# Two transformer blocks on one core: side work of the mixer placed between the dense projection blocks, and the second block's modulation moved into the feed-forward

## The chip, the cores and the metric

The kernel runs on one core of a Trainium2 chip. The metric is the device time of one execution in microseconds (us); lower is better. Engines are named as the profile names them: PE (TensorE, matmul), PEld (its weight load), DVE (VectorE), ACT (ScalarE), POOL (GpSimd), SP (SyncE, which here issues all DMAs).

## The reference

The input is x, 512 tokens by 1024 channels, f32. `first_block` runs two layers; `second_block` runs one.

```
for l in range(2):                                 # first_block
    proj = rms_norm(x) @ w_in[l]                    # latents a, group B, C + indexer, group D
    A: latents cq (256), ckv (128): rms_norm, up-projection, rope, causal attention, 4 heads
    B: q 4 heads, k and v 2 heads, rope, window of 128 keys with a sink per head
    C: I[t,s] = sum_h w[t,h] relu(q_idx[t,h].k_idx[s]), top 128 keys, attention over them
    D: causal attention with a forget gate, cum = cumsum(log_sigmoid(f))
    x = x + concat(A, B, C, D) @ w_out[l]
    x = x + square(relu(rms_norm(x) @ w_up[l])) @ w_down[l]
x = rms_norm(x) * final_norm
shift, scale, gate = split(c @ w_ada + b_ada)       # second_block
h = rmsnorm(x) * (1 + scale) + shift
proj = h @ w_in_2                                   # three qkv groups, z, u, z_pool, gates
three dilated window attentions with a bias table rel_bias[bucket], merged by their lse
pool mixer, gated branches, x + gate * (merged @ w_out), rmsnorm
```

## The kernel before

**Dense products.** Every weight matrix is cut into jobs of 1024 x 512, a job into two pieces (halves of K). SP loads a piece into one of 4 slots of `raw`; ACT rounds it to `w_hi` (helper `ahead`, `split_high`), POOL subtracts to get `w_lo` (`split_low`, L1107, two instructions of 128x1024 a piece), and PE makes three matmuls for each block (`three`, L1637 to L1639). `product` (one job) runs half 0 over four token tiles into four PSUM banks `G`, then half 1; each bank is handed to ACT or DVE as it fills. `w_hi` and `w_lo` have two places.

**Order.** Each engine has one program, and programs meet at counted semaphores; an engine never passes a wait. In a layer PE does: transposes of x; `project(JOB_IDX)` (296 columns), `project(JOB_A)` (420); three turns of the indexer rows; `project(JOB_C)`; `index_products(1)` and `(2)`, three turns of the latents; `project(JOB_B)`; `index_products(3)`, the latents' up-projections (L1739, L1743); `project(JOB_D)`; the cumulated gates (L1753); `project(JOB_V)`. Between two products PE waits for what the other engines make of its small results: for the indexer, ACT applies relu from PSUM to `rel` (two places) and DVE multiplies and adds into `select` (L1459, L1462). DVE also does all ropes (`rotate`), the 32 rounds of `top_round` for query tiles 1 and 2 (MAX8 and MATCH_REPLACE8, L1490 and L1491) and, beside the attention, the 16 rounds of query tile 3.

**Attention.** 32 items (8 head pairs in the order D, B, A, C, times 4 query tiles) run in a software pipeline: scores, maximum (DVE), exponential (ACT), scaling by 1/sum (POOL, L1116), transposes, copy, output. One top-k round for tile 3 follows each of the first 16 items on DVE.

**Feed-forward.** Four groups of four jobs in a hardware loop: two up jobs, ACT relu, DVE square and split, two down jobs whose banks DVE adds to X (`add_to_x`, L1603).

**Second block.** It opens with six jobs ADA (c broadcast to 128 rows times `w_ada`), between them 24 matmuls of the bias lines (L874) that ACT copies to `stage`; two norms of X one after the other (final norm of the first block, written to X; then the norm for `xn2`); transposes of `xn2`; `h_full` (ACT, scale and shift), its split into `h_hi`, `h_lo` (L668, L669); then the first qkv job. SP writes `stage` to DRAM (4.6 MB) and reads the skewed bias tables back.

Of the kernel before, what the change touches and what calls it, by code (L numbers as in the profile page):

```python
# [15 lines left out]
P = 128  # L16
# [9 lines left out]
HD = 64  # L26
# [24 lines left out]
JOB_IDX, JOB_A, JOB_C, JOB_B, JOB_D, JOB_V = range(6)  # L51
# [13 lines left out]
TR_MLA = TR_IDX + 3  # L65
TR_CUM = TR_MLA + 3
TR_NORM2 = TR_CUM + 2
# [3 lines left out]
PAIRS = [(g, hp) for g in "DBAC" for hp in range(2)]  # L71
# [4 lines left out]
def qk_units(p):  # L76

    return 4 if PAIRS[p][0] in "DA" else 2
# [23 lines left out]
IDX_PRODUCTS = 3 * 8  # L102
SM_EXP = 0
LAYER_SM = SM_EXP + 2 * TT
LAYER_SC = NI
LAYER_OV = NI
assert LAYER_TR % 2 == 0 and LAYER_TURNS % 2 == 0 and LAYER_SM % 2 == 0
# [39 lines left out]
ADA = 0  # L147
QKV = 6
Z_JOB, U_JOB, ZP_JOB = 15, 16, 17
GATE_JOBS = 18  # L150
BRANCH = 22
OUT2 = 24
# [4 lines left out]
SM2_BIAS = DEPTH * LAYER_SM  # L157
SM2_POOL = SM2_BIAS + B2_HEADS
# [30 lines left out]
TR2_MOD = TR0  # L189
TR2_NORM = TR2_MOD + 4  # L190
# [50 lines left out]
UNITS_CREDIT, PAIR_CREDIT, IDX_CREDIT = TT, 2, 4  # L241

# [29 lines left out]
def build(nc, A, out):  # L272
    ctx = ExitStack()
    with ctx:
        def sem(name):
# [8 lines left out]
        skew_dram = nc.dram_tensor("skew_scratch", [B2_HEADS, P, SKEW], F32, kind="Internal").ap()  # L284
        merge_dram = nc.dram_tensor("merge_scratch", [SEQ, PACK], F32, kind="Internal").ap()
# [19 lines left out]
        top8 = base.place("top8", [P, 8])  # L305
        neg_max = base.place("neg_max", [P, 2, 2])
# [23 lines left out]
        fox_q, fox_k = (room.place(n, [P, TT, HEADS, FOX_K]) for n in ("fox_q", "fox_k"))  # L330
        mla_q, mla_k = (room.place(n, [P, TT, HEADS, MLA_QK]) for n in ("mla_q", "mla_k"))
        mla_v = room.place("mla_v", [P, TT, HEADS * HD])
        dead_at = room.at
        w_uq, w_ukv = room.place("w_uq", [P, 2, HEADS * MLA_QK]), room.place("w_ukv", [P, HEADS * 2 * HD])
        k_idx4 = room.place("k_idx4", [P, TT, 4 * 32])
        qiT, kiT = room.place("qiT", [P, 2, SEQ]), room.place("kiT", [P, SEQ])
        select = room.place("select", [P, (2 + 3 + 4) * P])
        work, rel = room.place("work", [P, SEQ]), room.place("rel", [P, 2, SEQ])
        turn = room.place("turn", [P, 4, 8 * HD // 2])
# [6 lines left out]
        ident_few, window_few = room.place("ident_few", [P, P], BF16), room.place("window_few", [P, 2 * P], BF16)  # L346

# [3 lines left out]
        relu, square = room.place("relu", [P, 2, SEQ]), room.place("square", [P, SEQ])  # L351

        room = Room(nc, free_at)
        xn2 = room.place("xn2", [P, TT, D_MODEL])
        cb_hi, cb_lo = room.place("cb_hi", [P, KT, P], F32R), room.place("cb_lo", [P, KT, P], F32R)
        h_full = room.place("h_full", [P, 2, SEQ])
        hot = room.place("hot", [P, 3, SKEW])
        stage_at = room.at
        stage = room.place("stage", [P, B2_HEADS, SKEW])
        rel_wide = room.place("rel_wide", [P, B2_HEADS, P])  # L360
# [4 lines left out]
        assert room.at <= stage_at  # L365
        room = Room(nc, stage_at)
# [10 lines left out]
        assert room.at <= last_at  # L377
        room = Room(nc, last_at)
        gate_row, gain_row = room.place("gate_row", [P, D_MODEL]), room.place("gain_row", [P, D_MODEL])
        rel_row = room.place("rel_row", [P, B2_HEADS])  # L380
        mod_b, mod = room.place("mod_b", [P, 2 * KT]), room.place("mod", [P, 2 * KT])
        norm_col, c_col, pool_gain = (
            room.place(n, [P, k]) for n, k in (("norm_col", KT), ("c_col", KT), ("pool_gain", 4)))
# [21 lines left out]
        inv_ready, prob_scaled = sem("inv_ready"), sem("prob_scaled")  # L405
        small_filled, small_drained = sem("small_filled"), sem("small_drained")
# [5 lines left out]
        m_sumsq_ready, m_var_ready, m_std_ready, m_rows_ready = (  # L412
            sem(n) for n in ("m_sumsq_ready", "m_var_ready", "m_std_ready", "m_rows_ready"))
# [4 lines left out]
        heads_ready = sem("heads_ready")  # L418
        rel_used, neg_max_ready, hidden_split = sem("rel_used"), sem("neg_max_ready"), sem("hidden_split")
        dve_step = sem("dve_step")  # L420
        b2_loaded, gain2_loaded, c_ready = sem("b2_loaded"), sem("gain2_loaded"), sem("c_ready")
        rel_ready, skew_saved, bias_loaded = (
            sem(n) for n in ("rel_ready", "skew_saved", "bias_loaded"))
# [11 lines left out]
        def weights2(job, half):  # L435

            if job < QKV:
                w, c0, k0 = A["w_ada_2"], 512 * job, half * HALF_K
            elif job < Z_JOB:
# [17 lines left out]
        def second_loads(sp):  # L457
            sp.wait_ge(tr_drained, TR0 + PAIR_CREDIT)
            column = lambda v: v.rearrange("(k p) -> p k", p=P)
            for dst, src in (  # L460
                (c_col[:], column(A["c_2"][0, :])),
                (rel_row[0:NUM_BUCKETS, :], A["rel_bias_2"]),
                (gain_row[:], A["final_norm"].unsqueeze(0).broadcast_to([P, D_MODEL])),
                (norm_col[:], column(A["norm_g_2"][0, :])),
                (mod_b[:], column(A["b_ada_2"][0, 0:2 * D_MODEL])),
                (gate_row[:], A["b_ada_2"][0:1, 2 * D_MODEL:3 * D_MODEL].broadcast_to([P, D_MODEL])),
                (pool_gain[:], column(A["pool_scale_2"][0, :])),
                (inv_count[:], c_count[:, :, :]),
            ):
                sp.dma_start(dst, src, allow_slow_non_contiguous=True).then_inc(b2_loaded, 16)  # L470
            for job in range(OUT2 + 2):
# [4 lines left out]
                if job == 1:  # L476

                    sp.wait_ge(bank_drained, UNIT0 + UNITS_CREDIT)
                    sp.dma_start(hot[0:NUM_BUCKETS + 1], c_hot[:, :, :]).then_inc(hot_loaded, 16)
                if job == QKV:  # L480

                    sp.wait_ge(small_drained, SM2_BIAS + B2_HEADS + PAIR_CREDIT)
                    sp.dma_start(skew_dram.rearrange("h p u -> p h u"), stage[:]).then_inc(skew_saved, 16)
                    sp.wait_ge(x_scaled, 1)
                    sp.dma_start(gain_row[:], A["final_g_2"].unsqueeze(0).broadcast_to([P, D_MODEL])
                                 ).then_inc(gain2_loaded, 16)
# [3 lines left out]
                    sp.dma_start(bias_near[:], skewed(0, B2_H, 0, 2 * P)).then_inc(bias_loaded, 16)  # L490
                if job == QKV + 7:
# [21 lines left out]
        def second_scalar(act, split_high, square_sums, square_roots):  # L513
# [18 lines left out]
            def bias_rows(job):  # L532

                for h in range(4 * job, 4 * job + 4):
                    act.wait_ge(small_filled, SM2_BIAS + h + 1)
                    act.activation(stage[:, h, :], S[:, h % 2, 0:SKEW], ACT.Copy).then_inc(small_drained, 1)
# [7 lines left out]
            ahead(ADA + 1, 0)  # L544
            act.wait_ge(x_scaled, 1)
            square_sums(xn2)
            square_roots(DEPTH + 1)
            ahead(ADA + 1, 1)
            bias_rows(1)
            for job in range(2, QKV):  # L550
                ahead(job, 0)
                ahead(job, 1)
                bias_rows(job)

# [7 lines left out]
            for gn, g in enumerate(B2_GROUPS):  # L562
                for s in range(3):
                    job = QKV + 3 * gn + s
                    ahead(job, 0)
                    if gn == 0 and s == 0:
                        act.wait_ge(skew_saved, 16)
# [45 lines left out]
            square_roots(DEPTH + 2)  # L613

        def second_vector(dve, step, root, normal_rows):
            dve.wait_ge(b2_loaded, 8 * 16)

            wide = c_col[:].unsqueeze(2).broadcast_to([P, KT, P])
            step.done(dve.tensor_copy(cb_hi[:], wide))
# [33 lines left out]
            for ins in scaled_rows(2 * DEPTH, DEPTH):  # L653
                pass
# [1244 lines left out]
```

## Time and profile before

| | |
|---|---|
| median of 3 runs | 2209.36 us (2195.4 to 2210.68) |
| the profiled execution | 2206.09 us, its span 2204.1 us |
| granted PE clock, mean | 0.932 of full speed |
| PE / PEld busy | 1976.2 / 1568.6 us (90% / 71%) |
| DVE / ACT / POOL busy | 957.9 / 666.0 / 798.4 us |
| HBM read | 161.85 MB, 77 GB/s |

Busy times are sums over instructions and overlap between engines. [...] The first layer's projections lie at 22.4 to 198.6 us of the span, its attention up to 332 us, its feed-forward up to 744 us; the second layer repeats this up to 1470.5 us; the second block follows.

### The profile page before, as it was taken

The page shows a single profiled execution, that of the slowest core. Times are in us where ns is not written, and L with a number is a line of the kernel's source. Part 1 is how long each engine was busy: PE and PEld are TensorE (multiplying, and loading weights), DVE is VectorE, ACT ScalarE, POOL GpSimd, SP SyncE. Part 2 cuts the span into 40 slices and gives each one's busy share as a digit, 9 for nine tenths or more (in the row PEclk, how much of TensorE's full clock was granted, in tenths as well). Part 3 has the DMA queues.
Part 4 walks back from the last instruction along what each step waited for, and adds up shares of the span by engine and source line. Part 5 has one row for each costly group of instructions (what it writes and reads, how often), then busy time and mean ns, then how long its engine had stood idle before and what let it go on. Part 6 is the DMA issues. An engine that isn't in the chain of part 4 may idle for free.

```text
span 2204.1 us, 23720 instructions
## 1 busy us (share of the span) xinstructions
PE 1976.2 (90%) x9164; PEld 1568.6 (71%) x9168; DVE 957.9 (43%) x1704; ACT 666.0 (30%) x1167; POOL 798.4 (36%) x366
## 2 busy tenths in 40 slices
PE   7789889999999977988999999988889898788986
PEld 6556557878778855755777878765688786666765
DVE  3567842322323346875241422332111223756773
ACT  4333443312212342344231222234332323221211
POOL 4223233344444431323334444457331322132441
PEclk9888999999999988989999999998898888898998
DMA  6212001222222331200122222334631132031210
GB/s 191 75 39 77 1 1 58 96 92 91 84 95 79 89 108 39 69 9 1 41 94 95 95 79 94 113 98 153 229 96 37 40 116 77 2 100 57 96 58 38
DMA packets 109520, 170.89 MB, mean 78 GB/s; under 512 B 21724, under 2 KB 39388, under 8 KB 109309
## 3 DMA queue, kind: packets, MB, share of 16 engines
q1 hardware_dynamic: 109436, 169.76, 24.1%
q8 instruction: 55, 0.90, 0.2%
q14 instruction: 29, 0.23, 0.0%
HBM read 161.85 MB, written 7.90 MB: 77 GB/s over the span
## 4 chain that ended last, share of the span: by engine, by line
PE 62%; issue 14%; DVE 10%; POOL 10%; ACT 3%; SPq 1%; DMA 0%; DVEq 0%; POOLq 0%; ACTq 0%
PE G L1637 17%; PE G L1639 16%; PE G L1638 16%; POOL w_lo L1107 9%; PE S L1794 2%; PE G L1831 2%; PE G L1811 1%; PE G L921 1%; DVE qkv L771 1%; PE S L1679 1%; ACT prob L577 1%; POOL prob L1116 1%; PE G L907 1%; DVE select L1462 1%; PE G L1778 1%
## 5 line engine op out<-in xcount | busy, mean ns | idle before, releaser
L1107 POOL TENSOR_TENSOR w_lo<-raw,w_hi 128x1024 fp32r<-128x1024 f32 x296 | 721.0, 2458 | 1214.4 <-ACT w_hi L1144 753.0
L1637 PE MATMUL G<-h_hi,w_hi 128*128 128x512 f32 x896 | 361.0, 403 | 22.9 <-DVE qkv L772 11.6
L1144 ACT ACTIVATE w_hi<-raw 128x2048 fp32r<-128x2048 f32 x96 | 183.7, 1914 | 609.6 <-PE G L1639 609.6
L1638 PE MATMUL G<-h_lo,w_hi 128*128 128x512 f32 x896 | 358.6, 400 | 0.0
L1639 PE MATMUL G<-h_hi,w_lo 128*128 128x512 f32 x896 | 358.0, 400 | 0.0
L1637 PE MATMUL G<-w_hi,h_hi 128*128 128x512 f32 (+2 forms) x704 | 275.5, 391 | 17.0 <-DVE h_lo L777 8.2
L1639 PE MATMUL G<-w_hi,h_lo 128*128 128x512 f32 (+2 forms) x704 | 271.9, 386 | 0.0
L1638 PE MATMUL G<-w_lo,h_hi 128*128 128x512 f32 (+2 forms) x704 | 271.9, 386 | 0.0
L1637 PEld LDWEIGHTS G<-h_hi,w_hi 128*128 128x128 f32 x896 | 171.3, 191 | 68.3 <-DVE qkv L772 12.1
L1638 PE MATMUL G<-w_lo,u_hi 128*128 128x512 f32 x512 | 202.1, 395 | 0.0
L1639 PE MATMUL G<-w_hi,u_lo 128*128 128x512 f32 x512 | 202.1, 395 | 0.0
L1637 PE MATMUL G<-w_hi,u_hi 128*128 128x512 f32 x512 | 202.1, 395 | 0.0
L1639 PEld LDWEIGHTS G<-h_hi,w_lo 128*128 128x128 f32 x896 | 171.1, 191 | 42.1
L1638 PEld LDWEIGHTS G<-h_lo,w_hi 128*128 128x128 f32 x896 | 171.2, 191 | 41.4 <-issue 0.4
L525 ACT ACTIVATE w_hi<-raw 128x2048 fp32r<-128x2048 f32 x50 | 95.6, 1912 | 303.9 <-PE G L1639 287.7
L1603 DVE SCALAR_TENSOR_TENSOR X<-G,inv_square,X 128x512 f32<-128x512 f32 x64 | 48.1, 752 | 293.4 <-PE G L1639 293.4
L1637 PEld LDWEIGHTS G<-w_hi,h_hi 128*128 128x128 f32 x704 | 143.5, 204 | 40.8 <-DVE h_lo L777 8.7
L1638 PEld LDWEIGHTS G<-w_lo,h_hi 128*128 128x128 f32 x704 | 143.6, 204 | 22.0 <-issue 0.5
L1639 PEld LDWEIGHTS G<-w_hi,h_lo 128*128 128x128 f32 x704 | 142.8, 203 | 22.4
L1620 DVE TENSOR_TENSOR square<-relu 128x512 f32<-128x512 f32 x64 | 54.6, 852 | 207.5 <-ACT relu L1337 205.9
L1116 POOL TENSOR_TENSOR prob<-prob,inv_sum 128x256 f32<-128x256 f32 (+2 forms) x64 | 75.0, 1172 | 159.0 <-DVE inv_sum L1548 157.8
L1639 PEld LDWEIGHTS G<-w_hi,u_lo 128*128 128x128 f32 x512 | 96.3, 188 | 22.9
(279 smaller groups left out, 2496.4 us busy)
## 6 DMA issues: line engine op xcount, KB each, us to landing
raw<-in_w_in_dram SPq DMA_DIRECT2D x40, 1024.0 KB, 5.2
raw<-in_w_up_dram SPq DMA_DIRECT2D x32, 1024.0 KB, 5.3
raw<-in_w_down_dram SPq DMA_DIRECT2D x32, 1024.0 KB, 5.0
raw<-in_w_out_dram SPq DMA_DIRECT2D x12, 1024.0 KB, 5.0
raw<-in_w_ada_dram SPq DMA_DIRECT2D x12, 1024.0 KB, 5.1
skew_scratch<-stage SPq DMA_DIRECT2D x1, 4608.0 KB, 14.9
raw<-in_w_in_dram SPq DMA_DIRECT2D x8, 512.0 KB, 4.3
raw<-in_w_in_dram SPq DMA_DIRECT2D x4, 832.0 KB, 4.5
```

What stands on the lines that cost most here:

```text
L525: act.activation(w_hi[:, c % SPLIT_SLOTS], raw[:, c % RAW_SLOTS], ACT.Copy).then_inc(high_ready, 1)
L577: ins = act.activation(part[:, n, :], part[:, n, :], ACT.Exp, bias=head_neg[:, g, m, h:h + 1], accum_out=head_sum[:, g, m, h:h + 1])
L1107: ins = pool.tensor_tensor(w_lo[:, c % SPLIT_SLOTS, part], raw[:, c % RAW_SLOTS, part], w_hi[:, c % SPLIT_SLOTS, part].bitcast(F32), ALU.s ...
L1116: pool.tensor_tensor(part, part, inverse, ALU.mult).then_inc(prob_scaled, 1)
L1144: act.activation(w_hi[:, c % SPLIT_SLOTS], raw[:, c % RAW_SLOTS], ACT.Copy).then_inc(high_ready, 1)
L1603: dve.scalar_tensor_tensor(dst, G[:, t, :], factor, dst, ALU.mult, ALU.add).then_inc(bank_drained, 1)
L1620: step.done(dve.tensor_tensor(square[:], relu[:, n % 2, :], relu[:, n % 2, :], ALU.mult))
L1637: pe.matmul(dst, a_hi, b_hi, start=first, stop=False)
L1638: pe.matmul(dst, a_hi, b_lo, start=False, stop=False)
L1639: return pe.matmul(dst, a_lo, b_hi, start=False, stop=last)
L1794: pe.matmul(bank, qkT[at, p % 2, q, P * qt:P * qt + P], qkT[at, p % 2, k, P * tiles[0]:P * (qt + 1)], start=True, stop=False)
L1831: ins = pe.matmul(dst, values(p, e, kb), probT[:, i % 2, e, P * b:P * b + P], start=b == 0, stop=b == len(tiles) - 1)
```

## The change

- **Side work hosted in the products.** `product` takes a callback after each of its 32 positions (half, tile, k), 3 matmuls each. A generator `side()` on PE (and a twin on ACT) yields after each step; the table `HOSTED` says how many steps follow each position. Hosted are: indexer turns and six rounds of four products (in A from position 18, and in B up to 11), the latents L and their up-projections U (B), group B's q and k turns K (C, from 18), group B's eight attention items P (C, D, V), the gate sums F and the turns of B's output M (V). Job B now precedes job C.
- **Group B leaves the attention pipeline**: 24 items in the order D, A, C. B has its own path, all in the S banks: scores, maxima, exponentials, transposes back into the same bank, output with the probabilities as the stationary operand; DVE scales the output by 1/sum (POOL no longer does). The one top-k round per item for tile 3 stays with the first 16 items, which are now D and A.
- **DVE** runs a fixed list of steps with chores between them: rope of B and C in pieces, 32 early rounds spread over 23 steps. `rotate` uses two temporaries and three synchronised pairs in place of two.
- **Latents**: squares are taken by ACT from PSUM (scaled); the inverse root is applied to the up-projected rows.
- **Bias lines early**: in layer 0, between JOB_IDX and JOB_A, three matmuls give one line per head (8 rows); DVE copies them, SP writes them to DRAM and later broadcasts them DRAM to DRAM (4.7 MB) while the first layer's feed-forward starts.
- **Modulation summed on DVE**: in layer 1's feed-forward (loop unrolled for SP and DVE), 3 MB of `w_ada` come in per group, and in the six first of eight down tiles DVE does `ada_sum += w_ada * c` over 128x1024; at the end PE sums over partitions with `ones` (16 matmuls of one column, 2 of 512).
- **Two norms in one**: after each down tile of the last group DVE writes X * gain to `xn2`; ACT squares both X and `xn2` in halves (16 squares of 128x512); both inverse roots come from one pass. X itself is scaled after the splits of h.
- **SP order**: the loads of qkv job 1 and later stand behind `xn2_ready`, the bias loads and `x_scaled`.

```diff
-JOB_IDX, JOB_A, JOB_C, JOB_B, JOB_D, JOB_V = range(6)
+JOB_IDX, JOB_A, JOB_B, JOB_C, JOB_D, JOB_V = range(6)
-PAIRS = [(g, hp) for g in "DBAC" for hp in range(2)]
+PAIRS = [(g, hp) for g in "DAC" for hp in range(2)]
+SIDE = ([("L",)] + [("U", t) for t in range(TT)] + [("K",)]
+        + [("P", hp, qt) for hp in range(2) for qt in range(TT)] + [("F",), ("M",)])
+HOSTED = {JOB_IDX: {}, JOB_A: {18: 3, 21: 1, 25: 1, 29: 1},
+          JOB_B: {1: 1, 6: 1, 11: 1, **spread(12, 32, side_steps(0, AT["K",]))},
+          JOB_C: spread(14, 32, side_steps(AT["K",], AT["K",] + 3)),
+          JOB_D: spread(0, 32, side_steps(AT["K",] + 3, AT["K",] + 6)),
+          JOB_V: spread(0, 32, side_steps(AT["K",] + 6, NS + 1))}
...
# PE, product()
+                            if hosted:
+                                hosted(16 * half + HALF_K * t + kk)
...
# ACT
+                def host(job):
+                    for pos in range(32):
+                        if pos == 15:
+                            ahead(job, 0)
+                        if pos >= 16 and pos % 4 == 3:
+                            rows_out(job, pos // 4 - TT, rows_parts(job, pos // 4 - TT))
+                        for _ in range(HOSTED[job].get(pos, 0)):
+                            next(steps)
+                    ahead(job, 1)
...
+                        if n == 4 * ROOTS_ROUND + 3:
+                            latent_roots()          # Sqrt, Exp, Ln, each with its table
...
# DVE, layer 1's down jobs
+                        for t in range(TT):
+                            if last:
+                                add_modulation(g, TT * j + t)
+                            add_to_x(first, j, inv_square, [t])
...
+                    step.done(dve.scalar_tensor_tensor(ada_sum[:, at], w_ada[:, tile, at], c_col[:, k:k + 1], ada_sum[:, at],
+                                                       ALU.mult, ALU.add))
...
# ACT, start of the second block
-            square_sums(xn2, lambda t: act.wait_ge(bank_drained, UNIT0 + t + 1))
-            square_roots(DEPTH)
-            ahead(ADA, 0)
-            ahead(ADA, 1)
-            bias_rows(0)
...
+            for half in range(2):
+                at = slice(512 * half, 512 * half + 512)
+                for t in range(TT):
+                    act.wait_ge(scaled_ready, TT * half + t + 1)
+                    for n, rows in enumerate((xn2, X)):
+                        k = 2 * (TT * half + t) + n
+                        if k >= 2:
+                            act.wait_ge(half_squared, k - 1)
+                        act.activation(h_full[:, n, :], rows[:, t, at], ACT.Square,
+                                       accum_out=halves[:, half, n, t:t + 1]).then_inc(half_squared, 1)
```

## Rows read from the trace of the kernel before

**Rows 1.** Page, section 5: group, then busy us, mean ns, idle before and its releaser

```profile
L1144 ACT ACTIVATE w_hi<-raw 128x2048 fp32r<-128x2048 f32 x96 | 183.7, 1914 | 609.6 <-PE G L1639 609.6
```

**Rows 2.** Windows: length, PE, PEld, DVE, ACT, POOL busy us (instructions), clock, DMA, GB/s

```profile
22.40:198.60 176.20, 150.17 (x694) 119.97 (x692) 110.75 (x291) 63.80 (x107) 55.20 (x24) 0.89 0.25 79
...
1470.50:1565.10 94.60, 72.64 (x241) 48.27 (x241) 42.81 (x52) 51.41 (x64) 66.70 (x26) 0.83 0.47 155
1565.10:1636.30 71.20, 70.89 (x288) 61.07 (x288) 0.00 (x0) 16.20 (x17) 23.68 (x10) 0.96 0.57 180
...
233.80:264.00 30.20, 24.42 (x177) 16.38 (x175) 26.06 (x73) 14.78 (x57) 8.74 (x8) 0.94 0.00 1
264.00:293.50 29.50, 25.86 (x175) 17.80 (x174) 18.40 (x46) 13.03 (x45) 8.74 (x8) 1.00 0.01 1
```

**Rows 3.** Windows view, PE alone, of layer 0's projections: PE busy, clock, DMA share, GB/s

```profile
55.40:57.20 1.80, 1.45 (x14) 1.00 1.00 377
57.20:79.40 22.20, 22.20 (x103) 1.00 0.31 98
79.40:101.90 22.50, 7.98 (x46) 0.58 0.18 56
...
124.80:149.80 25.00, 14.36 (x40) 0.73 0.16 50
...
172.30:174.40 2.10, 2.10 (x22) 1.00 0.25 95
174.40:198.60 24.20, 24.16 (x98) 0.93 0.25 77
```

**Rows 4.** Timeline, DVE beside POOL: start us, us, instruction, idle before and releaser

```profile
82.25 2.26 DVE L1459 TENSOR_SCALAR select<-rel,rows_idx 128x256 f32<-128x256 f32 x1 [12.91 <-ACT rel L1230]
...
82.03 4.69 POOL L1107 TENSOR_TENSOR w_lo<-raw,w_hi 128x1024 fp32r<-128x1024 f32 x2 [6.73 <-ACT w_hi L1144]
...
164.84 0.56 DVE L1490 MAX8 top<-work 128x8 f32<-128x384 f32 x1
...
163.50 4.79 POOL L1107 TENSOR_TENSOR w_lo<-raw,w_hi 128x1024 fp32r<-128x1024 f32 x2 [31.22 <-ACT w_hi L1144]
```

**Rows 5.** Timeline, PE: four index products of 512 keys; one up-projection to the next

```profile
124.79 1.14 PE L1719 MATMUL S<-kiT,qiT 32*128 32x512 f32 x8
...
145.94 1.45 PE L1739 MATMUL S<-w_uq,cqT 128*128 128x384 f32 x4
...
148.09 1.45 PE L1739 MATMUL S<-w_uq,cqT 128*128 128x384 f32 x4
```

**Rows 6.** Timeline, PE: scores and transposes of a B item, outputs of eight 64-column matmuls

```profile
261.61 0.70 PE L1794 MATMUL S<-qkT 64*128 64x256 f32 x4
...
262.81 0.66 PE L1811 MATMUL G<-masks,prob 128*128 128x128 f32 x4 [0.18 <-POOL prob L1116]
...
1651.48 1.90 PE L921 MATMUL G<-qkv,probT 128*128 128x64 f32 x16
```

**Rows 7.** Timeline, DVE: the first half of a top-k round beside a B item

```profile
265.57 0.69 DVE L1490 MAX8 top<-work 128x8 f32<-128x512 f32 x1
```

**Rows 8.** Groups of the stretch 1470.4 to 1565.1: columns as in rows 1

```profile
L1152 ACT ACTIVATE xn<-X 128x1024 f32<-128x1024 f32 x8 | 8.3, 1042 | 0.0
...
L1157 ACT ACT_TABLE_LOAD x1 | 1.3, 1283 | 0.0
```

**Rows 9.** Timeline, DVE, end of the feed-forward and the splits of h

```profile
1470.50 0.75 DVE L1603 SCALAR_TENSOR_TENSOR X<-G,inv_square,X 128x512 f32<-128x512 f32 x1 [2.05 <-PE G L1639]
1471.16 0.68 DVE L619 CAST cb_hi<-c_col 128x1024 fp32r<-128x1024 f32 x1
1471.88 1.23 DVE L620 TENSOR_TENSOR cb_lo<-c_col,cb_hi 128x1024 fp32r<-128x1024 f32 x1
...
1557.96 0.69 DVE L669 TENSOR_TENSOR h_lo<-h_full,h_hi 128x512 fp32r<-128x512 f32 x1
...
1559.03 0.69 DVE L669 TENSOR_TENSOR h_lo<-h_full,h_hi 128x512 fp32r<-128x512 f32 x1
```

More of the change, by code:

```diff
@@ L1 @@
 from contextlib import ExitStack
+import itertools
 import math
@@ L1092, in _ @@
                         sp.dma_start(raw[:, slot], src).then_inc(raw_loaded[slot], 16)
+                        if c == 4 and l == DEPTH - 1:
+                            sp.wait_ge(ada_free, g + 1)
+                            rows = slice(ADA_TILES * g * P, ADA_TILES * (g + 1) * P)
+                            sp.dma_start(w_ada[:], A["w_ada_2"][0, rows, :].rearrange("(k p) n -> p k n", p=P)
+                                         ).then_inc(ada_loaded, 16)
+                if l == DEPTH - 1:
+                    for g in range(FFN_GROUPS):
+                        group_loads(g)
+                        if g == 0:
+                            second_params(sp)
+                else:
+                    with sp.Fori(0, FFN_GROUPS) as g:
+                        group_loads(g)
             second_loads(sp)
@@ L1385, in low_T, with rotate @@
                                              ALU.mult, ALU.subtract).then_inc(tr_drained, 1)
-            def rotate(v, table, heads, half):
-                for t in range(TT):
+            def rotate(v, table, heads, half, tiles=range(TT)):
+                for t in tiles:
                     x1, x2 = v(t)[:, :, 0:half], v(t)[:, :, half:2 * half]
@@ new lines, in _ @@
+                log_forget()
+                for n in range(NS + 1):
+                    if n and "t" in units(n - 1)[0]:
+                        take_more(n - 1)
+                    if n < NS:
+                        start(n)
+                    if n and SIDE[n - 1][0] == "P":
+                        window_sums(n - 1)
+                    if continues(n):
+                        chores(n, False)
+                    if n and SIDE[n - 1][0] == "P":
+                        window_output(n - 1)
+                        chores(n, True)
@@ new lines, in window_output @@
+                def window_output(n):
+                    pe.wait_ge(even_taken, evens + (EVEN[n, "t"] + 1))
+                    pe.wait_ge(odd_taken, odds + (ODD[n, "t"] + 1))
+                    tiles = window_tiles(n)
+                    for e in range(2):
+                        for b, kb in enumerate(tiles):
+                            ins = pe.matmul(bank(n, 0)[:, HD * e:HD * e + HD], prob_b[n % 2][e][:, P * b:P * b + P],
+                                            rows_b[:, kb, 384 + HD * e:384 + HD * e + HD], start=b == 0, stop=b == len(tiles) - 1)
+                    ins.then_inc(side_even, 1)
@@ L1701, in _ @@
+                steps = side()
                 pe.wait_ge(bank_drained, unit + (UNITS_CREDIT + 1 - TT))
```

945 lines of the change are left out of this document (563 added, 382 removed).

## The prediction, as it was put on record

> **What bounds the kernel now.** I read the windows view first, in stages cut, then the chain of waits, then the timelines of single engines. The chain is mostly PE, but that share hides two kinds of stage. In the dense ones PE is full: a 512-column job takes 22.2 us with PE busy for all of it [rows 3]. In the others PE waits. Layer 0's projections last 176.2 us with PE busy for 150 [rows 2], and the rest sits in the interludes between jobs: 1.8, 22.5, 25.0 and 2.1 us [rows 3], 51.4 us together, with the clock granted at 0.58 and 0.73 in the two long ones. The second layer repeats the pattern. The other thin stage is the 94.6 us between the last feed-forward matmul and the first qkv product, where PE works mostly on what the change removes [rows 2]. DVE is the engine to watch: 110.8 us busy in the projections, and not free when it is idle. Beside a POOL split a DVE instruction of 256 elements took 2.26 us and ended as the first of the two POOL instructions did, while MAX8 beside the next split of this kind ran its normal 0.56 us [rows 4].
>
> **The second block's opening.** Removed: all of the 94.6 us. What follows the last down product now is a chain, counted from the last matmul. ACT must first round the next piece, 1.9 us [rows 1], since `ahead` stands before the squares in its program. Then 16 squares of 128x512, none of which it can start earlier: a square of 1024 takes 1.04 us [rows 8], and for 512 I estimate half plus 0.09 for the accumulator, 0.61; 16 make 9.8. The square root's table, 1.3 [rows 8], covers DVE's sums. Root and five small DVE steps: 1.2 (estimate). Scaling four rows of 1024 at 0.7, like the cast of that size, and the two gate additions at 0.75, like `add_to_x` [rows 9]: 4.3. Four transposes 0.7 [rows 6], the ACT pass of one slice 0.8 (near the DVE pass of rows 9). Four slices of h at a pitch of 1.07 [rows 9]: 4.3. The last transposes of slice 7 stand before the product: 0.7. Sum 25.0, gain 69.6 us. The 16 one-column matmuls and two of 512 are new; bounds are 1 us (column time only) and 10 us (16 at the price of a four-transpose group). Both end before the squares do, so I count nothing; if that cover went, up to 5 us would show. Bounds of the gap: 18 us, if the squares overlapped the last product, and 40 us, if each DVE step paid a POOL instruction.
>
> SP's order is the trap here. The loads of qkv job 1 now wait for `x_scaled`, which DVE gives after all eight slices and four 1.23 us passes [rows 9], some 9 us after qkv job 0 begins. Load, ACT 1.9 and POOL 4.8 [rows 1, 4] follow and end near 21 us, just inside a job of 22 to 24. Before, the three jobs ran in 71.2 us with PE busy 70.9 [rows 2] behind a similar wait, so I cost it at zero; without cover it is a few us, once.
>
> **The modulation in the feed-forward.** 24 two-input passes of 1.23 us [rows 9], 29.5 us of DVE, plus multiplications of the last group. Each stands ahead of an `add_to_x` of 0.75, in a rhythm of one bank every 2.8 us (22.2 us a job, eight half-tiles). Four tiles need 8 us of 11.1; with two holds by a POOL split of 2.4 us each [rows 4] up to 12.7. The lag is taken back: the next job needs the last bank only 8 us later, and the last group's final tiles have no modulation. DMA adds 12 MB over four groups but drops the same 12 MB from the opening, and the loads run four pieces, 44 us, ahead. SP waits for `ada_free` about until the piece behind is split anyway. Cost zero; uncovered, 24 holds of 2.4 us are 58.
>
> **The projections, per layer.** PE work that moves inside the products, at full clock: nine turns of four (index, L, K) and two for M at 0.66 [rows 6], 7.3 less 0.5 for pairs; six index rounds, the longest 1.14 [rows 5], 5.5; four up-projections at 2.15 from one to the next [rows 5], 8.6; F 2.1 [rows 3]; eight B items. A B item is scores 0.70, transposes 0.66, four output matmuls 0.95 (half of rows 6's eight), masks 0.3 (estimate): 2.4 without overlaps, 19 in all. Sum 42. Bounds are 36 and 50, the latter at partly half clock.
>
> Stalls that stay, because each PE step waits in place and holds the product behind it. Index round 4 (in B) waits for round 3: ACT first rounds a piece (1.9), then DVE's first two steps of the round are held by the two POOL instructions (4.8), against 3.5 us of product cover (five positions of 0.7): 4.6. Then `latent_roots` puts three tables (3 x 1.3) before round 4's relus: 3. Round 5 and L: 2.1. Smaller handshakes: 2.5. Together 12. For C, D and V, DVE has per item with rope pieces: a maximum of about 0.7 and small steps, 2.8 rounds of about 1.2, two rope pieces of 1.5 and copies, 8.7 us; PE gives it 9.8. With 4.8 us per split, partly under immune rounds, DVE falls behind in D and recovers in V: 8. Total 20; bounds 0, and 40 from the idle that the interludes show now plus what group B's handshakes could add.
>
> Returned: the last job runs at 24.2 against 22.2 [rows 3], 2.0. So the projections change by 51.4 + 2.0 - 42 - 20 = 8.6 us slower each. Layer 0 also waits for the bias lines: three f32 matmuls and a DVE copy of 1152 columns, 3.5 us on the path.
>
> **The attention, per layer.** Group B's stretch of 30.2 us goes [rows 2]. Its DVE rounds do not: about ten rounds of two passes of 0.69 us [rows 7], 1.4 each, fall on A, whose stretch has 29.5 us with DVE busy 18.4 and PE 25.9 [rows 2]. With them DVE has 30 or more and becomes the bound, so A grows by 4.5 us (bounds 1 and 10). Gain 25.7. Netted, a layer gains 17.1.
>
> **Sum.** 2 x 17.1 - 3.5 + 69.6 = 100 us. The profiled execution took 2206 us (3 below the median of 2209), so 2106 us.
>
> [...] The rows show that the holding of DVE by POOL is real but selective [rows 4]. [...]
>
> **Rivals.**
> 1. *The hosting is smooth*: stalls 5 instead of 20 per layer, because 36% of DVE's work is immune and the steps lie apart. 2106 - 30 = 2076. For it: PE is full in 22.2 us jobs with DVE's slack beside them. Against: the three tables and the round-3 hold have no cover.
> 2. *DVE becomes the bound of the projections.* DVE work there is about 105 us with group B, the splits hold up to 12 x 4.8 = 57 more, and PE has 163. If nothing immune lies under the splits the two are equal and every order constraint shows: stalls 40 per layer, 2146. [...]
> 3. *The modulation delays the down jobs*, by its full 58 us: 2164. Against: the lag is recovered within a job.
> [...]
> 5. *The opening stays long and the stalls are at their bound*, so that almost nothing is left: about 2190.
>
> [...]
>
> **Chances.** Forecast 0.50 (its own range 2086 to 2126), rival 1 0.22, rival 2 0.17, rival 3 0.04, rival 4 0.03, rival 5 0.04. A measurement of this kernel can tell about 1%, 22 us, from no change. Faster 0.93, same 0.04, slower 0.03. Range 2068 to 2148: it takes in rivals 1 and 2 with their bounds.
>
> **What would show it.** Gap to the first qkv product 25 us, with ACT squares as its longest part. Projections 182 to 190 us a layer, with PE waits named ACT `rel` and DVE inside job B, and few in C. Attention 107 us, DVE nearly full beside group A. Feed-forward of layer 1 unchanged at 22.4 us a job. [...]

## The result, and the profile after

The changed kernel takes **2111.95 us** (median of 4 runs, 2110.48 to 2118.62), the kernel before 2206.80 on the same chip: ratio 0.9584, 95% interval 0.9542 to 0.9626. Forecast were 2106 (2068 to 2148) and "faster". The profiled execution took 2111.23 us with a span of 2109.4, against 2204.1: 94.7 us gained where the sum had 100.

The windows view, cut where the stages now begin and end (columns as in [rows 2]): projections of layer 0 and 1, feed-forward of layer 1 up to the last down matmul, the gap to the first qkv product, and group A's stretch of the attention.

```profile
21.80:212.40 190.60, 171.88 (x852) 134.81 (x850) 130.50 (x339) 80.55 (x165) 59.28 (x26) 0.94 0.32 101
738.10:922.60 184.50, 164.85 (x848) 130.00 (x847) 129.06 (x338) 80.71 (x165) 56.81 (x25) 0.97 0.22 72
1030.60:1443.90 413.30, 409.43 (x1763) 328.93 (x1763) 178.67 (x181) 95.12 (x86) 183.76 (x70) 1.00 0.33 115
1443.90:1469.10 25.20, 13.61 (x69) 9.93 (x68) 12.12 (x30) 17.62 (x41) 4.67 (x2) 0.59 0.25 69
249.90:281.30 31.40, 26.80 (x196) 18.77 (x194) 25.36 (x60) 13.41 (x43) 10.02 (x8) 1.00 0.01 2
```

Beside [rows 2], the gap of 94.6 us is 25.2, the projections are longer (176.2 to 190.6 in layer 0) though the interludes are gone, because PE busy rose from 150 to 172: work of other stages is in there. B's stretch of 30.2 is gone, and A's went from 29.5 to 31.4. In the table a stretch ends where the next begins: the projections run from their first product matmul to the attention's first matmul, so they are 176.9 us before, 0.7 more than the window of [rows 2] that ends with the last product.

| stretch | change forecast | change measured |
|---|---|---|
| second block's opening | -69.6 | -69.4 (94.6 to 25.2) |
| projections, layer 0 | +8.6 + 3.5 | +13.7 (176.9 to 190.6) |
| projections, layer 1 | +8.6 | +8.4 (176.1 to 184.5) |
| attention, layers 0 and 1 | -25.7 each | -25.1, -23.4 (to 108.1 and 108.0) |
| feed-forwards | 0 | -0.5, +0.9 |
| second block after its opening, start of the kernel | 0 | +1.3, -0.6 |

What PE waited for in layer 1's projections (the view of waits: who, for what, us in total, times, longest):

```profile
PE G L2077 <- DVEq L1705: 5.4, 1, 5.4
PE S L1931 <- ACT rel L1279: 5.2, 2, 4.3
PE S L2034 <- DVE prob_b L1647: 3.5, 1, 3.5
PE S L1958 <- ACT rel L1279: 1.7, 1, 1.7
PE S L2020 <- DVE qkT_b L1649: 1.1, 1, 1.1
PE S L1989 <- issue: 0.9, 1, 0.9
PE S L1890 <- DVE k_idx L1668: 0.8, 1, 0.8
```

With four smaller ones that is 19.5 us, forecast 20 (19.1 in waits of 0.3 us and more; sums of waits below count these). Three meetings of DVE with POOL's split stand behind the largest. DVE is held there: its step is recorded as several times its usual length while POOL's instruction runs. First the round before index round 4; the timeline of ACT, POOL and DVE (start, length, instruction):

```profile
778.13 1.93 ACT L1200 ACTIVATE w_hi<-raw 128x2048 fp32r<-128x2048 f32 x1
780.13 5.00 POOL L1163 TENSOR_TENSOR w_lo<-raw,w_hi 128x1024 fp32r<-128x1024 f32 x2 [11.95 <-ACT w_hi L1200]
780.47 6.52 DVE L1683 SCALAR_TENSOR_TENSOR select<-rel,w_idx,select 128x384 f32<-128x384 f32 x4 [2.66 <-ACT rel L1279]
787.86 1.28 ACT L1267 ACT_TABLE_LOAD   x1
...
881.60 4.83 POOL L1163 TENSOR_TENSOR w_lo<-raw,w_hi 128x1024 fp32r<-128x1024 f32 x2 [12.01 <-ACT w_hi L1200]
881.73 2.48 DVE L1487 TENSOR_TENSOR turn<-rows_c,rope 128x128 f32<-128x128 f32 x1
884.24 2.34 DVE L1488 TENSOR_TENSOR rows_c<-rows_c,rope 128x128 f32<-128x128 f32 x1
888.59 0.29 DVE L1647 COPY prob_b<-S 128x128 f32<-128x128 f32 x1
...
919.72 4.76 POOL L1163 TENSOR_TENSOR w_lo<-raw,w_hi 128x1024 fp32r<-128x1024 f32 x2 [13.50 <-ACT w_hi L1200]
919.98 2.29 DVE L1525 TENSOR_SCALAR select<-work 128x384 bf16<-128x384 f32 x1
```

Four steps that need 0.62 each take 6.5 beside the first split, and PE waits 4.3. In job V two rope steps of 0.29 take 2.48 and 2.34 beside the next one, and the copy for which PE waits (3.45) stands behind them. The last, at the end of V, holds the mark of tile 2 (about 0.3 free, an estimate from DVE steps of this size), behind which stands `heads_ready`: 5.4, of which the hold explains 2; the rest is DVE's backlog of rounds, which experiment 3 takes away. The forecast had said that DVE falls behind in D and recovers in V; it does not recover.

A wait costs more than itself. PE right behind the one in V:

```profile
888.94 1.11 PE L2034 MATMUL S<-rows_b,prob_b 128*128 128x64 f32 x4 [3.45 <-DVE prob_b L1647]
...
890.39 0.63 PE L1846 MATMUL G<-w_lo,h_hi 128*128 128x512 f32 x1
890.81 0.63 PE L1847 MATMUL G<-w_hi,h_lo 128*128 128x512 f32 x1
...
892.38 0.39 PE L1845 MATMUL G<-w_hi,h_hi 128*128 128x512 f32 x1
892.61 0.39 PE L1846 MATMUL G<-w_lo,h_hi 128*128 128x512 f32 x1
```

The starts of these products, 512 columns each, are 0.43 us apart until 892, where the clock was granted at 0.50, then 0.23, at 1.00.

The gap, in the timeline of all engines:

```profile
1443.96 1.91 ACT L1200 ACTIVATE w_hi<-raw 128x2048 fp32r<-128x2048 f32 x1 [9.28 <-PE G L1847]
1445.78 0.61 ACT L612 ACTIVATE h_full<-xn 128x512 f32<-128x512 f32 x1
1447.25 2.46 PE L901 MATMUL S<-ada_sum,masks 128*128 128x512 f32 x4
...
1455.68 1.28 ACT L615 ACT_TABLE_LOAD   x1
...
1458.27 0.75 DVE L699 TENSOR_SCALAR xn<-xn,rstd 128x1024 f32<-128x1024 f32 x1
...
1464.48 0.69 DVE L708 TENSOR_TENSOR h_lo<-h_full,h_hi 128x512 fp32r<-128x512 f32 x1
...
1469.12 0.48 PE L1845 MATMUL G<-h_hi,w_hi 128*128 128x512 f32 x1
```

1.9 for the piece [rows 1], squares to 1455.7 (9.9), the table of 1.28 [rows 8], 1.3 for roots and small steps, then scaling and slices: the chain as worked out, 25.2 against 25.0. PE's sums of the modulation (3.63 us for the 16 of one column, then the line shown) end at 1449.7, 6 us before the squares.

### The profile page after: what moved, and what is told of

Same layout as the page of the kernel before. It is cut to its first block, busy times and chain, and to the rows that moved or that the text cites. A ratio compares the mean times of both kernels' runs of the same rounds, so it can differ in the third digit from the quotient of the medians.

```text
span 2109.4 us, 23190 instructions
## 1 busy us (share of the span) xinstructions
PE 1910.5 (91%) x9010; PEld 1522.4 (72%) x9010; DVE 1004.1 (48%) x1717; ACT 631.9 (30%) x1140; POOL 736.3 (35%) x326
## 4 chain that ended last, share of the span: by engine, by line
PE 59%; issue 15%; DVE 13%; POOL 9%; ACT 2%; SPq 1%; DMA 0%; DVEq 0%; POOLq 0%; ACTq 0%
PE G L1845 15%; PE G L1847 15%; PE G L1846 15%; POOL w_lo L1163 8%; PE S L2093 2%; PE G L2128 2%; PE G L951 1%; DVE qkv L813 1%; PE G L2110 1%; DVE select L1683 1%; PE G L2077 1%; ACT prob L636 1%; POOL prob L1172 1%; PE S L925 1%; DVE work L1521 1%
## 5 line engine op out<-in xcount | busy, mean ns | idle before, releaser
L1163 POOL TENSOR_TENSOR w_lo<-raw,w_hi 128x1024 fp32r<-128x1024 f32 x272 | 673.8, 2499 | 1204.8 <-ACT w_hi L1200 750.6
L1845 PE MATMUL G<-h_hi,w_hi 128*128 128x512 f32 x896 | 359.8, 402 | 19.8 <-DVE qkv L814 11.6
L1200 ACT ACTIVATE w_hi<-raw 128x2048 fp32r<-128x2048 f32 x96 | 183.8, 1914 | 562.4 <-PE G L1847 562.4
L1845 PE MATMUL G<-w_hi,h_hi 128*128 128x512 f32 (+2 forms) x704 | 284.2, 404 | 17.7 <-DVE h_lo L819 8.2
L597 ACT ACTIVATE w_hi<-raw 128x2048 fp32r<-128x2048 f32 x38 | 72.6, 1911 | 275.9 <-PE G L1847 261.7
L1846 PEld LDWEIGHTS G<-w_lo,u_hi 128*128 128x128 f32 x512 | 96.1, 188 | 25.0
L1845 PEld LDWEIGHTS G<-w_hi,u_hi 128*128 128x128 f32 x512 | 96.1, 188 | 23.0
```

What stands on the lines that cost most here:

```text
L597: act.activation(w_hi[:, c % SPLIT_SLOTS], raw[:, c % RAW_SLOTS], ACT.Copy).then_inc(high_ready, 1)
L1163: ins = pool.tensor_tensor(w_lo[:, c % SPLIT_SLOTS, part], raw[:, c % RAW_SLOTS, part], w_hi[:, c % SPLIT_SLOTS, part].bitcast(F32), ALU.s ...
L1200: act.activation(w_hi[:, c % SPLIT_SLOTS], raw[:, c % RAW_SLOTS], ACT.Copy).then_inc(high_ready, 1)
L1845: pe.matmul(dst, a_hi, b_hi, start=first, stop=False)
L1846: pe.matmul(dst, a_hi, b_lo, start=False, stop=False)
```

## The experiments

Each is an edit of the changed kernel; ratios are to the kernel before on the same chip. Stretches come from each run's trace.

**1. All steps behind the last product of their job.**

```diff
+HOSTED = {job: {31: sum(at.values())} if at else {} for job, at in HOSTED.items()}
```

> The same steps in the same jobs, but all of a job's steps stand behind its last product instead of between its products. Theory (the hosted steps are cheap because products cover the waits between them): PE's own hosted work, about 43 us a layer, stays, and the waits come back: some 30 us a layer of index and latent interludes as in the kernel before, and about 2.5 us for each of group B's eight items, against 19 us of stalls now. That makes 30 to 40 us a layer more, 2175 to 2195 us, with a granted clock that falls in the waits. Rival (the gain came from the new order and from taking group B out of the attention, the places between products matter little): within 15 us of 2112.

2197.30 us, 0.9956 [0.9941, 0.9972]; projections 232.3 and 223.4 us.

```profile
23.00:255.00 232.00, 190.17 (x852) 147.34 (x850) 122.23 (x339) 82.00 (x165) 56.43 (x25) 0.82 0.26 83
```

Layer 0 lost 41.7 us: PE's waits went from 18.3 to 41.1, and PE busy from 171.9 to 190.2 for the same 852 instructions, at a clock of 0.82 instead of 0.94. The total is 2 us above the theory's range, and only half of the loss is waiting; the other half goes with the clock, which is lower in this stretch. The two layers lose 41.7 and 38.9 us, the attention of layer 1 another 5.9; the medians differ by 85 us. This kernel keeps the opening's 69 us and most of the attention's gain; projections that last 55 and 47 us longer than in the kernel before take nearly all of it back. So without the places between the products the change is worth 0.4%.

**2. No modulation in the feed-forward.**

```diff
-                    step.done(dve.scalar_tensor_tensor(ada_sum[:, at], w_ada[:, tile, at], ...))
```

> The 24 additions into ada_sum in the second layer's feed-forward are left out (their loads stay), so scale, shift and gate come from the bias alone. Theory (the lag of DVE is taken back within a job): no change, 2108 to 2113 us, feed-forward of layer 1 at 412 to 413 us. Rival 3 in part (a part of the 58 us of held additions shows): 2055 to 2105 us, and waits of PE on DVE X in the last feed-forward gone.

2110.14 us, 0.9563 [0.9520, 0.9607]: no difference that can be told. The feed-forward of layer 1 has 413.3 us with and without, and PE waits 3.1 us there for the X that DVE updates in both, so these waits aren't the modulation's. In the changed kernel the 24 additions (groups by line: busy, mean ns) were:

```profile
L1824 DVE SCALAR_TENSOR_TENSOR ada_sum<-w_ada,c_col,ada_sum 128x1024 f32<-128x1024 f32 x24 | 53.3, 2220 | 0.1
```

The shortest took 1.28, the mean 2.22: POOL held them, and PE saw none of it. The loads of `w_ada` were kept, so this run doesn't test them.

**3. Without 30 of the 32 early rounds.**

```diff
-                        top_round(1 + r // ROUNDS, r % ROUNDS)
+                        if r % ROUNDS == 0:
+                            top_round(1 + r // ROUNDS, 0)
```

> 30 of the 32 top-k rounds beside the products of each layer are left out (the chosen keys are then wrong), some 33 us of DVE a layer. Theory (DVE's backlog makes the stalls of D and V and the wait at the end, 3.45 and 5.38 us): those go, index stalls stay, 8 to 9 us a layer, 2094 to 2097 us. Rival (the backlog is only POOL's hold): the D stall stays near 3 us and the last wait falls by the one held step, 2.3 us: 2106 to 2108 us. Second rival (DVE is the bound of the whole stage): also the stalls in job B go, 2075 us.

2086.81 us, 0.9463 [0.9428, 0.9498]; projections 179.2 and 177.5. PE's longest waits in layer 1:

```profile
PE S L1932 <- ACT rel L1279: 4.7, 2, 4.3
PE S L1891 <- DVE k_idx L1669: 3.2, 1, 3.2
```

The 3.45 and the 5.38 are gone and the index stalls stand: the first theory's mechanism. But 25 us went instead of 16, so its range was missed. The projections gained 11.4 and 7.0 us, of which 8.2 and 6.3 are waits; the rest is PE's pace. The attention after them was shorter too, 103.3 and 105.8 against 108, at a granted clock of 0.93 and 0.92 instead of 0.87.

The 3.2 for the indexer rows instead of 0.85 stands also in the profiles of experiments 5, 6 and 9, whose edits don't touch it. It is a race. DVE's copy of the index weights, which stands ahead of the copy that PE waits for, met POOL's next split here:

```profile
748.85 2.34 POOL L1163 TENSOR_TENSOR w_lo<-raw,w_hi 128x1024 fp32r<-128x1024 f32 x1 [4.33 <-ACT w_hi L1200]
748.87 2.35 DVE L1668 COPY w_idx<-rows_idx 128x32 f32<-128x32 f32 x1
```

In these four profiles POOL's instruction starts 0.02 to 0.03 us ahead of the copy, which takes 2.35 us. In both profiles of the changed kernel and in those of experiments 2, 7 and 11 it starts 0.12 to 0.15 us behind it, and the copy takes 0.18. So 2.3 us of a profile's layer 1 can be chance.

**4. POOL's split in four instructions.**

```diff
-                for k in range(0, HALF_K, 2):
-                    part = slice(k, k + 2)
+                for k in range(HALF_K):
+                    part = slice(k, k + 1)
```

> POOL subtracts each piece in four instructions of 128x512 instead of two of 128x1024. Theory (a DVE step with two SBUF inputs waits for the end of one POOL instruction, then has its turn): the hold is 1.2 us instead of 2.4, so four DVE steps pass beside a split where two passed; round 4's stall falls from 4.3 to about 2.7 us, D's from 3.45 to about 1.9, the last wait by 1.1: 4 us a layer, 2103 to 2106 us. Rival (the hold lasts until POOL is through with the piece, or POOL's extra instructions cost as much): 2110 to 2116 us.

2113.33 us, 0.9586 [0.9555, 0.9616]: no change. Layer 1's waits show why:

```profile
PE S L1931 <- ACT rel L1279: 6.3, 2, 4.1
PE G L2077 <- DVEq L1705: 4.3, 1, 4.3
PE S L2034 <- DVE prob_b L1647: 3.3, 1, 3.3
```

Round 4's wait fell from 4.3 to 2.1 as expected, but round 5's rose from 0.9 to 4.1. Counted from the end of ACT's rounding, the shorter holds let PE's round 4 start 2.2 us sooner, but DVE's four sums beside the four POOL instructions still took 6.01 us (6.52 in the changed kernel), and the latent roots with their table loads, which stand ahead of round 4's relus on ACT, wait for DVE behind these sums. So the relus came only 0.5 us sooner. Their wait had been hidden behind round 4's stall: the hold was a cover. The trace has two table loads there, Exp and Ln, 1.28 us each, not three; the square root of these rows ran without one.

**5. Without 15 of the 16 rounds of tile 3.**

```diff
-                    if i < ROUNDS:
+                    if i == 0:
                         top_round(3, i)
```

> 15 of the 16 top-k rounds of query tile 3, which DVE runs beside the attention items of D and A, are left out in each layer (the keys chosen for that tile are then wrong). Theory of the prediction (these rounds make DVE the bound of A's stretch): the attention falls by about 4.5 us a layer, 108 to 103.5, 2101 to 2104 us. Rival (DVE is busy for only 25 of A's 31 us, so the rounds lie in its idle time, and the attention's length follows the granted clock): 0 to 1.5 us a layer, 2108 to 2112 us.

2104.80 us, 0.9558 [0.9533, 0.9583]. A's stretch:

```profile
249.90:279.10 29.20, 26.34 (x196) 18.62 (x194) 14.69 (x36) 13.43 (x43) 10.04 (x8) 1.00 0.01 2
```

2.2 us shorter in both layers, D's 1.2 and 0.8 (the whole attention 102.7 and 106.2, the rest of it moving with the clock): neither the forecast's 4.5 nor nothing. DVE was busy for 25.4 of 31.4 us with the rounds, so it isn't the bound; a round stands in the way of single steps. In the changed kernel:

```profile
240.69 0.68 DVE L1520 MAX8 top<-work 128x8 f32<-128x512 f32 x1
...
242.20 0.69 DVE L1714 TENSOR_SCALAR qkT<-G 96x512 f32<-96x512 f32 x1
...
242.94 1.08 PE L2077 MATMUL G<-masks,mla_k 128*96 128x128 f32 x8 [1.49 <-DVE qkT L1714]
```

PE waits 1.49 for a copy of A's turned rows that stands behind a round, in D's stretch, and 1.27 for the next such copy in A's. Both waits are gone without the rounds.

**6. Squares early, the piece rounded last.**

```diff
 # ACT, last group of the feed-forward
+                        if end:
+                            halves_squared(act, 0, range(TT))
                         ahead_g(job, 0)
+                        if end:
+                            halves_squared(act, 1, range(TT))
-                        ahead_g(job, 1)      # now after the eight slices of h
```

> ACT takes the squares of the first half beside the last down product and those of the second as its tiles come, and rounds the second piece of the first qkv job after the eight slices of h instead of first. Theory (the gap of 25.2 us is ACT's chain, 1.9 for the piece and 16 squares of 0.61): it ends with the last tile's two squares, so the root comes some 8 to 9 us earlier; what is late next is PE's sums of the modulation, 6.1 us after the last product. Gap 16.5 to 18 us, 2103 to 2105 us. Rival (POOL's split of the piece, now behind the slices, and the rounding that comes 27 us later delay the first qkv job's second half, or the sums of the modulation bound the gap above 20 us): less than 4 us gained, 2108 us or more.

2111.71 us, 0.9586 [0.9557, 0.9615]: nothing, as the rival had it. The gap is 19.8, 5.4 less, but the second block after it is 6.4 longer, and what is late next shows twice.

```profile
1451.37 0.17 DVE L696 TENSOR_TENSOR mod<-S,mod_b 128x16 f32<-128x16 f32 x1 [4.05 <-PE S L904]
...
1466.98 9.15 DVE L788 SCALAR_TENSOR_TENSOR X<-X,rstd,gain_row 128x1024 f32<-128x1024 f32 x4
1467.69 6.17 POOL L1166 TENSOR_TENSOR w_lo<-raw,w_hi 128x1024 fp32r<-128x1024 f32 x2 [27.80 <-ACT w_hi L1203]
...
1491.01 0.80 PE L1866 MATMUL G<-h_hi,w_hi 128*128 128x512 f32 x1 [4.71 <-POOL w_lo L1166]
```

DVE waits 4.05 for PE's sums, whose cover was the squares. Then the four scalings of X meet the moved split and take 9.15 instead of 4.87; behind `x_scaled` wait SP's loads of the second qkv job, and PE waits 4.7 for its `w_lo`.

**7. New order in the projections**: the line's wait moved to the first hosted step; rounds 2, 1 and 0 to a step; the tables after the first turn of the latents; rounds 4 and 5 two positions later.

```diff
+ROUNDS_AT = [2] * 12 + [1] * 8 + [0] * 3
-          JOB_B: {1: 1, 6: 1, 11: 1, **spread(12, 32, ...
+          JOB_B: {1: 1, 8: 1, 13: 1, **spread(14, 32, ...
-                        if n == 4 * ROOTS_ROUND + 3:
-                            latent_roots()
+                        if n == 0:               # side step L
+                            latent_roots()
-                    pe.wait_ge(line_ready, 1)    # now in side(), l == 0
```

> Four changes of order in the projections: PE waits for the copy of the bias lines only at the first hosted step; the 32 early rounds are put two to a step in the first 12 steps, one in the next 8, none in the last three; the three ACT tables of the latent roots come after the first turn of the latents instead of in the middle of the index rounds, and the inverse roots after them; rounds 4 and 5 stand two positions later. Theory (each wait has the cause that the trace names): the line's wait 1.4, the wait at the end 5.4 to about 1, D's 3.5 to 1 to 2, the waits of round 5 and of the latents 2.5 to 0, with round 4 at 3 to 4: 8 to 10 us a layer and some for half-speed matmuls behind the waits, 2090 to 2096 us. Rival (a stall taken away comes back at the next meeting, as the split in four showed when round 4 gained 2.0 and round 5 lost 3.3): 2104 to 2112 us.

2098.00 us (2088.17 to 2102.97), 0.9519 [0.9481, 0.9558], 2 us above the theory's range; projections 185.4 and 176.5. The wait at the end fell from 5.4 to 0.9, those of round 5 and of the latents from 2.5 to 0, the 3.45 became 2.2 and round 4's 2.9. Layer 0 gained only 5, because it has a new wait of 6.14 for the indexer rows. The DVE timeline there:

```profile
49.52 2.45 DVE L1491 TENSOR_TENSOR rows_idx<-rows_idx,rope 128x144 f32<-128x144 f32 x1
52.01 2.33 DVE L1492 TENSOR_TENSOR rows_idx<-rows_idx,turn 128x144 f32<-128x144 f32 x1
```

PE without its wait, and with its first products 0.19 us apart where they were 0.35 behind the wait, ends the job's first half sooner. The next split starts at 49.45 instead of 51.68, DVE's ropes stand 0.9 us later, and one step of each of the last two rope pairs runs into it.

**8. Experiments 4, 6 and 7 together.**

> The new opening, the new order of the projections and POOL's split in four instructions together. Theory (the savings lie in different stretches and add, and round 4's stall is shorter with the shorter hold): 2112 - 8 - 18 - 3, 2080 to 2088 us. Rival (each comes back elsewhere): 2095 us or more.

2084.32 us (2082.15 to 2087.26), 0.9467 [0.9441, 0.9494], inside the theory's range. Against the changed kernel's 2112 the three gave 0, 0 and 14 us alone and give 28 together, so this is more than their sum. The waits show where: round 4's is 0.8 us, so the shorter hold pays once the tables are out of its way, and PE's wait for `w_lo` behind the opening is 2.6 (two waits) where experiment 6 had 4.7. The sums of the modulation still come 3.5 us late.

**9. Experiment 6 without what gave it back, with the changed kernel again.**

```diff
-                    sp.wait_ge(x_scaled, 1)              # at job QKV, now at QKV + 7
-                    sp.dma_start(gain_row[:], ...)
+            ins.then_inc(mod_filled, 1)                  # PE, after the 16 column sums
-                if t == 0:
+                if t == 1:
+                    dve.wait_ge(mod_filled, 2)
```

> The changed kernel again, unchanged, beside the next three, so that they have their reference on the same chip. Every theory: 2108 to 2116 us, the gap of the opening 25.2 us and the stalls of the projections as in its first profile.

2116.37 us (2109.03 to 2120.95), 0.9591 [0.9560, 0.9622], gap 25.3, waits 19.4 and 19.1. The projections of layer 0 lasted 188.7 us against 190.6 in the first profile, those of layer 1 184.4 against 184.5.

> The opening of the previous experiment, with two orders changed: SP loads the last norm's gain (and so waits for the scaled X) seven jobs later instead of ahead of the loads of the second qkv job, and the 16 column sums of the modulation are announced before the two wide ones, the gate's sum standing behind the second row tile. Theory (the shorter gap was given back because SP's loads stood behind the scaled X, whose four passes POOL's split now holds to 9.2 us: PE waited 4.7 us for w_lo, and DVE waited 4.1 us for the sums): gap 17 to 18 us, no wait for w_lo in the second qkv job, 7 to 8 us less than the changed kernel, 2103 to 2106 us. Rival (the second qkv job is late because ACT rounds the first job's second piece last): a wait for w_lo of 2 us or more stays, 2107 us or more.

2106.51 us (2105.86 to 2107.36), 0.9550 [0.9526, 0.9573]. The gap is 17.8, DVE's wait for the sums is down to 0.4 and none for `w_lo` is left, so the causes were these two:

```profile
1446.40:1464.30 17.90, 14.12 (x64) 10.24 (x65) 12.30 (x31) 8.56 (x17) 0.00 (x0) 0.66 0.44 122
```

The 7.4 us of the gap are in the trace. The medians differ by 9.9 us, but the intervals of the two kernels overlap, so the whole time alone couldn't show them.

**10. All of it**: experiment 8 with the orders of 9.

> The same opening together with the new order of the projections and POOL's split in four. Theory (the savings add): 2084 less 2.6 for the w_lo waits seen in the combination and 2.2 for the sums, 2077 to 2081 us. Rival (something else is late next): 2083 us or more.

2083.79 us (2076.43 to 2085.12), 0.9440 [0.9412, 0.9467]. Its profile has the gap at 16.1 and layer 1's projections at 170.0 with a clock of 1.00:

```profile
731.10:901.10 170.00, 161.45 (x847) 128.11 (x846) 126.40 (x338) 79.08 (x165) 58.29 (x45) 1.00 0.25 79
```

3.2 and 3.7 less than in 8, but the attention of layer 1 took 111.2 against 107.1. The projections' share is no gain of the edit: PE's waits there are the same (8.3 and 8.4 us), and the granted clock was 0.98 in experiment 8; the attention's loss goes with a clock of 0.85 against 0.89. The theory's 2077 to 2081 was missed, and the rival's bound of 2083 holds for the median. It is the fastest kernel here, 33 us under the changed one on the same chip; 8 can't be told from it.

**11. Experiment 7 with the line's wait where the change has it.**

> The new order of the projections, but PE waits for the copy of the bias lines where the changed kernel has it, behind the three matmuls. Theory (moving that wait brings nothing, since the indexer rows are then 6.1 us late: DVE's ropes run into the POOL split that PE's earlier first half has started): layer 0's wait of 1.4 is back, its wait for the indexer rows 0 to 0.9, projections of layer 0 at 182 to 184 us against 185.4, 2 us faster than with the move. Rival (the wait for the rows has nothing to do with where the split falls): the 6.1 stay and 1.4 come on top, 187 us in layer 0.

2090.97 us, 0.9481 [0.9450, 0.9511]; projections of layer 0 at 178.0, layer 1 at 173.4. The waits of layer 0:

```profile
PE S L1933 <- ACT rel L1281: 2.9, 1, 2.9
PE S L2022 <- DVE rows_b L1664: 2.9, 2, 2.2
PE G L1847 <- DVE line L1515: 1.4, 1, 1.4
```

The 6.1 us are gone with 1.4 put back: a wait that delays PE kept DVE's ropes clear of a split, as the theory said. Layer 0 is 7.4 us shorter where 2 were expected; 4.4 of that are waits, 3.0 PE's pace. Layer 1, which has the same program and the same waits in both, also differs by 3.1, so such a difference of pace shows nothing of the edit, and the intervals of the two kernels overlap. Experiments 8 and 10 have the moved wait (4.8 us there); neither was run without it.

## Why the prediction was right, and where it was off

- **Opening**: right in length and in chain. The PE sums counted at nothing took 6 us under the squares (bounds 1 and 10), and experiment 6 showed the price of the lost cover as named, 4.05 against "up to 5".
- **SP's order**: counted zero, measured 0.5. X was scaled 8.3 us after the product began (9 forecast), but the load took 7.6, so `w_lo` came at 23.1, not 21: at the edge of the job. Experiments 6 and 9 show the edge from both sides.
- **Modulation**: zero, as said (experiment 2). The holds are real, 24 additions longer by 0.94 each, 23 us where the uncovered bound had 58.
- **Projections**: +8.4 for 8.6 in layer 1, in part by luck, since the terms were off and cancel. The index part had 8.9 of waits against 12: the hold before round 4 cost 4.3 (4.6 forecast), tables, round 5 and L 2.5 against 5.1. The forecast counted three table loads where the trace has two, and it added the hold and the tables, which cover each other (experiment 4). C, D and V had 10.3 against 8, in another place: no wait of 0.3 us lies in D, and half of the sum is the end of V. Hosting's own work is 184.5 less 19.5 of waits and 120.7 of products (96 matmuls of 296 columns at 0.137 apart, 96 of 420 at 0.190, 384 of 512 at 0.2325), which leaves 44.3; 5.9 of that are product matmuls at half speed, which the forecast didn't count, so it is 38 against 42. Layer 0 lasted 6.1 and 4.3 us longer than layer 1 in the two profiles of the changed kernel. The lines cost 3.5 of that between the products, as said; the half-speed matmuls right behind their wait, ten at 0.35 apart instead of 0.19 in the first profile, add 1.7, which wasn't counted.
- **Attention**: the largest miss of the sum, 2.9 us over both layers, and here even that nearness is luck. Taking B out gave its 30.2. The 4.5 of A was the step that failed: DVE was not the bound, and eight rounds fall on A, not ten. A grew by 1.8, of which experiment 5 takes away all (2.2). What the forecast had at nothing made up for it: D grew by 2.2, since A's turns, which before stood in B's stretch, now stand in D's: mostly a turn more (1.0) and the wait of 1.49. The granted clock in D was 0.74 against 0.72 before, so it isn't the cause. The first turns behind the 5.4 us wait, at a clock of 0.56, took 0.8 more, and C 0.3 and 2.0.
- **POOL's hold of DVE**, taken from [rows 4], carried the right terms: in the trace a held DVE step ends with the POOL instruction it met (2.48 us for 0.29), and the next meets the second (2.34); of two that start within 0.15 us the one that was first ran through, in nine profiles (experiment 3). POOL was held as well, 6.17 us beside four DVE scalings for 4.7 alone (experiment 6). What makes the two hold each other was not shown. Experiment 4 showed that the length of the POOL instruction isn't the price by itself.
- **Rivals**: 1 (smooth, 2076) was wrong for this order, yet experiment 11, which changes places and order alone, takes 2091, 21 us under the changed kernel's first median and 25 under the one on its own chip, where the rival stood 30 under the forecast. Nearly half of the waits were a matter of places (19.5 to 10.5 us in layer 1). 2 (2146) needed stalls of 40; DVE was busy for 130 of 190 us. 3 falls with experiment 2. 4, products slowed by a clock that falls in the waits, never decides: the projections were granted 0.94 and 0.97. But experiment 1 shows it at work: PE was busy 18 us longer a layer, at 0.82 and 0.84. 5 (2190) falls with the gap of 25.2.

## What to carry to other kernels

Small work hosted between the products of a dense job costs its own PE time (38 us in layer 1 here), the waits whose cover is too short (19.5), and some half-speed matmuls behind them (5.9); read each wait's releaser, then ask what DVE met just before, above all another engine's hold on it. Stalls on one chain cover each other, so they are neither added in a forecast nor removed one at a time: the two that did nothing alone, the shorter hold and the shorter opening, were worth it in company. Compare waits, not lengths: with the same waits a stretch of 175 us differed by 3 to 4 us between profiles. After each such edit look where the split or load that the bounding engine triggers now falls.

## What the runs showed of the hardware

- A POOL instruction is held as well: two of 128x1024 took 6.17 us beside four DVE scalings (4.7 alone), and in experiment 4 four of 128x512 took 5.92 beside DVE's index sums (1.29 each is their median).
- DVE operations with one SBUF input were held too: the mark (128x384 f32 to bf16) 2.29 us beside a split, and a copy of 128x32 f32 2.35 us for 0.18 when POOL's instruction had started 0.02 us ahead of it. MAX8 and MATCH_REPLACE8 of 128x384 ran at 0.54 to 0.56 throughout.
- The wait of 3.45 us inside dense work was followed by 2.3 us of product matmuls 0.43 us apart instead of 0.23, at a granted clock of 0.50, and in the stage with 41 us of waits (experiment 1) the same instructions kept PE busy 18 us longer, at a granted clock of 0.82 instead of 0.94.
- An f32 matmul left two records, a matmul of the split products one: 32 for the 16 one-column sums, 8 for four index products [rows 5], 3 for the three products of a position. Neighbouring records overlap: product matmuls of 512 columns are recorded as 0.39 us long and start 0.23 apart.
- A sum over partitions by a one-column f32 matmul took 0.23 us: 16 of them 3.63 us.
- Changing ACT's function table cost the load of 1.28 us and no more: after the load at 787.86 the next function ran at 789.15.
